# Moving the subtraction that makes the weights' low halves from GpSimd to VectorE for the first 44 weight units of a layer

## The reference

```python
h = rms_norm_2(x, norm_mix[l])
z = h @ w_in[l]                       # 1024 x 4768, split in nine
c_q, c_kv, k_pe, hq, hf, hi, hg, g_a, g_b = jnp.split(z, offsets, axis=-1)
y_a = mla_mixer(c_q, c_kv, k_pe, ...) @ w_proj_a[l]      # causal attention, 8 heads
y_b = hgrn2_mixer(hq, hf, hi, hg, ...) @ w_proj_b[l]     # gated linear recurrence, 4 heads
x = x + (sigmoid(g_a) * y_a + sigmoid(g_b) * y_b) @ w_out[l]
h = rms_norm_2(x, norm_ffn[l])
x = x + (silu(h @ w_gate[l]) * (h @ w_up[l])) @ w_down[l]
```

## Time and profile before

| | |
|---|---|
| Timed runs, median of three | 3962.72 us |
| The profiled execution's own time | 3969.89 us |
| Its span, first to last instruction | 3968.2 us |
| TensorE matmul busy | 3658.0 us, 92% |
| VectorE busy | 2035.3 us, 51% |
| ScalarE busy | 864.3 us, 22% |
| GpSimd busy | 1391.4 us, 35% |
| Mean granted TensorE clock | 0.956 |

### The profile page before, as it was taken

One profiled execution on the slowest core, in us unless ns is written; L12 is line 12 of the kernel. 1 busy time (PEld: TensorE's weight loads), 2 busy tenths in 40 slices (PEclk: granted clock), 3 DMA queues, 4 the chain that ended last, 5 costly groups with the idle time before them and its releaser, 6 DMA issues. The chain is left out here.

```text
span 3968.2 us, 45876 instructions
## 1 busy us (share of the span) xinstructions
PE 3658.0 (92%) x18494; PEld 2942.3 (74%) x18494; DVE 2035.3 (51%) x3165; ACT 864.3 (22%) x1690; POOL 1391.4 (35%) x602
## 2 busy tenths in 40 slices
PE   7897978999999989977999799899999898899998
PEld 3684567888887879956888566688888576788887
DVE  5797543224337556674233356864243367853342
ACT  3213412110002243311100244431000344422001
POOL 2321043225555200005455322235445322245454
PEclk9898889999999999988999899899999899999999
DMA  5443312221113100013332232123332221223322
GB/s 170 149 149 130 130 43 69 64 64 54 54 48 93 52 14 1 2 63 90 96 100 91 59 82 54 48 61 101 98 97 80 67 75 48 54 80 91 98 93 80
DMA packets 400350, 306.79 MB, mean 77 GB/s; under 512 B 11228, under 2 KB 367782, under 8 KB 399559
## 3 DMA queue, kind: packets, MB, share of 16 engines
q1 hardware_dynamic: 398040, 303.37, 25.3%
q10 hardware_dynamic: 2095, 0.44, 0.1%
HBM read 297.48 MB, written 6.29 MB: 77 GB/s over the span
## 5 line engine op out<-in xcount | busy, mean ns | idle before, releaser
L422 POOL TENSOR_TENSOR low<-raw,high 128x1024 fp32r<-128x1024 f32 (+1 forms) x437 | 1053.7, 2412 | 1491.9 <-DVE high L346 1491.9
L487 PE MATMUL scores<-high 128*128 128x512 f32 (+1 forms) x1944 | 741.3, 381 | 85.8 <-POOL low L422 64.0
L487 PE MATMUL scores<-low,high 128*128 128x512 f32 (+1 forms) x1944 | 728.1, 375 | 0.0
L487 PE MATMUL scores<-high,low 128*128 128x512 f32 (+1 forms) x1944 | 726.8, 374 | 0.0
L346 DVE CAST high<-raw 128x1024 fp32r<-128x1024 f32 (+1 forms) x437 | 399.8, 916 | 499.2 <-PE scores L487 267.9
L487 PE MATMUL bank<-high 128*128 128x512 f32 (+1 forms) x1480 | 541.5, 366 | 0.2
L487 PE MATMUL bank<-low,high 128*128 128x512 f32 (+1 forms) x1480 | 538.8, 364 | 0.0
L487 PE MATMUL bank<-high,low 128*128 128x512 f32 (+1 forms) x1480 | 538.0, 364 | 0.0
L487 PEld LDWEIGHTS scores<-high 128*128 128x128 f32 x1944 | 376.7, 194 | 163.9 <-POOL low L422 68.4
L487 PEld LDWEIGHTS scores<-high,low 128*128 128x128 f32 x1944 | 375.0, 193 | 65.7
L487 PEld LDWEIGHTS scores<-low,high 128*128 128x128 f32 x1944 | 376.5, 194 | 62.9 <-issue 1.0
(11 more groups left out here) (628 smaller groups left out, 5361.6 us busy)
## 6 DMA issues: line engine op xcount, KB each, us to landing
raw<-in_mlp_w SPq DMA_DIRECT2D x128, 512.0 KB, 3.9
raw<-in_w_in SPq DMA_DIRECT2D x76, 512.0 KB, 3.9
ring<-in_ada_w SPq DMA_DIRECT2D x32, 1024.0 KB, 7.3
raw<-in_w_gate SPq DMA_DIRECT2D x44, 512.0 KB, 3.8
raw<-in_w_up SPq DMA_DIRECT2D x44, 512.0 KB, 3.8
raw<-in_w_down SPq DMA_DIRECT2D x40, 512.0 KB, 3.4
mix<-in_ada_w SPq DMA_DIRECT2D x16, 1024.0 KB, 7.4
raw<-in_od_w_in SPq DMA_DIRECT2D x29, 512.0 KB, 3.8
```

The lines of the kernel that those rows point to most:

```text
L422: pool.tensor_tensor(tile(low, u), tile(raw, u), tile(high, u).bitcast(F32), ALU.subtract)\
L487: mm = pe.matmul(out(p), stationary, moving, start=(k0 + k == 0 and i == 0), stop=(k0 + k == job.kc - 1 and i == len(pairs) - 1))
```

## The change

VectorE gets a parameter `low_by_vector`. For the units below it VectorE makes the low half itself, directly behind the cast, and GpSimd leaves them out. The second block's layers set it to 44, all other uses keep 0. Six of those 44 units are native, so 38 subtractions a layer move, 76 in all. The counters `high_ready` and `low_ready` count as before.

```diff
@@ def products(...)
-             before=None, loads=(), sides=(), banks=8, sums=None):
+             before=None, loads=(), sides=(), banks=8, sums=None, low_by_vector=0):
@@ def halve_weights(dve, u)
             dve.tensor_copy(tile(high, u), tile(raw, u)).then_inc(high_ready, 1)
+            if u < low_by_vector:
+                dve.wait_ge(high_ready, halved(u))
+                dve.tensor_tensor(tile(low, u), tile(raw, u), tile(high, u).bitcast(F32), ALU.subtract)\
+                    .then_inc(low_ready, 1)
@@ def lower_weights(u)        # GpSimd
-                if not native[u]:
+                if not native[u] and u >= low_by_vector:
                     pool.wait_ge(high_ready, halved(u))
@@ layer_products(...)
-        before=before, ring_tiles=3, sides=[...], sums=...)
+        before=before, ring_tiles=3, low_by_vector=44,
+        sides=[...], sums=...)
```

More of the change, by code:

```diff
@@ L3880, in layer_products @@
             written_by=15, room=halves, room_after=13, lead=6)],
-        before=before, ring_tiles=3, sides=[constants, prep, attention, forget, levels, gates, states, norm], sums=SquareSums(m, x, toks))
+        before=before, ring_tiles=3, low_by_vector=44,
+        sides=[constants, prep, attention, forget, levels, gates, states, norm], sums=SquareSums(m, x, toks))
 def program(nc, A, out):
```

## The result

| | before | after |
|---|---|---|
| Median of five runs each | 3960.19 us | 3981.40 us |
| Range | 3958.61 to 3968.01 | 3980.65 to 3991.16 |
| Profiled span | 3968.2 us | 3979.0 us |
| VectorE / GpSimd busy | 2035.3 / 1391.4 us | 2080.3 / 1208.5 us |

The ratio is 1.0053, 95% interval 1.004 to 1.0065: slower, by 21.2 us. 3982 us was forecast, +19.6.

The account below looks back on a forecast made before the run. VectorE's order of work was taken to set TensorE's pace. Per layer -0.6 + 0 + 3.8 + 6.1 + 0.5 = +9.8, for two layers +19.6 us, so a median of 3982 us; range 3963 to 3997 us.

Parts of the forecast that it names:

- The bound: Attention and levels: VectorE's order of work sets TensorE's pace; no listed wait of TensorE is on GpSimd's subtraction L422.
- The price: Each moved subtraction puts 1.26 us into VectorE's stream, 48 us a layer for 38, before cover and relief.
- Head: Units 0 and 1: the last activation half starts earlier and runs shorter, -0.6 us a layer.
- Preparation: Units 2 to 18, turns up to 16: VectorE mostly waits, so 0 us, bounds -1.5 and +1.5.
- Attention: Turns 17 to 29: only turns 19, 23 and 27 pass on 1.26 us each, +3.8 us a layer.
- Levels: Turns 30 to 41, units 32 to 43: added work less relief and hidden parts, +6.1 us a layer.
- casts 32 to 39: First part of the levels' list, VectorE's casts of these units: +2.0 us of the levels' +6.1.
- casts 40 to 43: Last part of the levels' list, VectorE's casts of these units: +4.1 us of the levels' +6.1.
- relief: Levels: VectorE instructions stretched beside GpSimd's subtractions shorten, up to 6.7 us a layer; rival that this wins: 3947 us, 0.09.
- Clock: Attention: TensorE's longer idle stretches may make its granted clock sag, +0.5 us a layer.
- The clock case: Rival: granted clock falls in attention and levels, 5 and 3 us a layer, 16 in all; 3998 us, chance 0.12.

Follow-up runs that it names:

- three: Against the kernel before: VectorE makes the low halves of units 21, 25 and 29 alone, three a layer; 3979.32 us, 1.0037.
- other_twelve: Against the kernel before: VectorE makes the low halves of units 17 to 20, 22 to 24, 26 to 28, 30 and 31 alone; 3963.83 us, 0.9996.
- fill: The kernel before with 2, 3 and 3 extra matmuls on TensorE in turns 19, 23 and 27, results never read; 3959.56 us, 0.9984.
- fill_two: The kernel before with 2, 3 and 3 unread matmuls in turns 19, 23 and 27, and VectorE making units 33 and 34's low halves; 3953.68 us, 0.9974.

## Why the prediction was right

- **The bound.** TensorE waits on VectorE's order of work, not on GpSimd: right. No long wait on GpSimd went away behind unit 0, where TensorE's wait on L422 (6.48 us) only became one on VectorE's subtraction (5.32), and every grown wait ends on VectorE or on ScalarE behind it.
- **The price, 1.26 us.** Right: 1.87 us from cast to mask, and the median of the 76 subtractions is 1.23. The row that I gave for instructions that read PSUM (L3180 at 2413.61) starts before GpSimd's subtraction at 2413.77; the ones at 2414.66 and 2415.84 us, wholly beside it, take the same 0.29.
- **Head, -0.6 us.** Small and in the right direction: unit 1 starts 0.35 us sooner from VectorE's first scaling. I counted the last half only; TensorE also waited 1.46 us for an earlier one.
- **Preparation, 0.** -0.2 us.
- **Attention, +3.8.** The mechanism and the turns are right (14.2 - 10.4 us of waits; three carries all, other_twelve nothing).
- **Levels, +6.1.** +5.3 / +5.9. By part: unit 31 to 38 holds the effect of casts 32 to 39 (39 is made at 2559.39 us, before unit 38 starts), forecast +2.0, measured +1.7 / +2.3; unit 38 to 44 that of casts 40 to 43, forecast +4.1, measured +3.6 / +3.6. Price and relief each measured near their sums, and the whole is known to about 1 us: against the average of the six kernels that leave the levels alone, 129.5 us, it is +5.3.
- **Clock, +0.5.** The term that was mis-sized. It was +2.4 / -0.2 us in attention, 1.1 on average, by the two profiles, and about 2.2 by all of them. I wrote that the clock "may sag" and took no price from a row; the three units behind those waits, at 7.1 to 7.3 us or 5.7, would have given one: 1.4 to 1.6 us each. The total hides it because the levels came out 0.5 to 0.9 us lower. That 3982 us met 3981.4 so closely is in part luck: the loss itself is only known to be 16 to 26 us.
- **Rivals.** The clock case was right in kind, but far from its size (2.2 us by the two profiles, 4.4 by the averages, of 16). The relief is worth 6.3 to 6.9 us a layer in the levels, less than the 12.5 to 14.0 us that the work costs which bought it. VectorE's `TENSOR_SCALAR` takes 0.54 us alone, 0.68 beside GpSimd's 0.63 us instruction and 2.59 beside one of 2.55; GpSimd's own time hardly changes (2.55, against 2.40 on average in the kernel before). The Trainium skill has the rule that GpSimd's instructions and VectorE's two-port ones block each other (Advanced Engine Details and Errata, VectorE Performance Modes). The trace agrees on VectorE's side; which of VectorE's instructions are two-port ones no row tells.

## What to carry to other kernels

When work moves to an engine whose order is fixed, list its turns and look in each for a wait between the new instruction and the next one that somebody wants; the turns without a wait pay in full, the others nothing, and the engine's busy share tells neither. Before taking work off an idle engine, check whose wait ends on it: in attention and the levels nobody's did. And where TensorE must wait a few microseconds in any case, matmuls that nobody reads are worth trying: here eight a layer gave 4 us of 3960, as much as the two best-placed subtractions.

## What was not expected of the hardware

- Eight extra matmuls a layer, 2.7 us for three of them, placed inside waits, shortened the stretch around them by 3.2 us (139.5 to 136.28), since the granted clock stayed at 1.00.
- The same stretch (unit 17 to 31) with the same work took 139.46 and 140.96 us in the two layers of one execution, with two and three half-speed units. With the clock held, all four such stretches of fill and of fill_two agree within 0.01 us. The scatter there is the clock's.
- VectorE's small instruction of 128 x 512 took 2.59 us beside GpSimd's 128 x 1024 subtraction of 2.55, and 0.68 beside one of 0.63 us (128 x 128). Both times it began 0.23 us after GpSimd's instruction and ended 0.27 or 0.28 us after it, so the length of GpSimd's instruction set the price.
